# Two transformer blocks on one core: the modulation ahead of the first weights, three norm factors behind the products, and filler matmuls in front of waits

## The reference, cut to what matters

```python
mod = c_act @ w_mod + b_mod                       # 1024 x 6144; shift, scale and gate of two norms
h = rms_norm(x, norm_mix) * (1.0 + scale_m) + shift_m
z = h @ w_in                                      # first block: xr, yr, qa, ...
...
h = h + hybrid_mixer(rmsnorm(h, g_mix), ...)      # second block, layer 0 and 1; ends in y @ w_mix_out
q = rmsnorm(h, g_x) @ w_xq                        # cross attention to a memory of 256 rows, 4 heads of 256
p = softmax(q @ k.T * 256 ** -0.5);  h = h + (p @ v) @ w_xo
hn = rmsnorm(h, g_ffn)
h = h + (silu(hn @ w_gate) * (hn @ w_up)) @ w_down          # layer 0: a dense feed-forward of width 2816
h = h + sum of two chosen experts of eight, width 3584      # layer 1
```

## Time and profile before

| | us |
|---|---|
| three executions | 2289.72, 2297.3, 2298.78 |
| median | 2297.3 |
| profiled execution | 2299.69, span 2298.0 |
| mean granted TensorE clock | 0.975 of full |

### The profile page before, as it was taken

One profiled execution on the slowest core, in us unless ns is written; L12 is line 12 of the kernel. 1 busy time (PEld: TensorE's weight loads), 2 busy tenths in 40 slices (PEclk: granted clock), 3 DMA queues, 4 the chain that ended last, 5 costly groups with the idle time before them and its releaser, 6 DMA issues.

```text
span 2298.0 us, 34432 instructions
## 1 busy us (share of the span) xinstructions
PE 2179.6 (95%) x13775; PEld 1954.0 (85%) x13775; DVE 1743.8 (76%) x1916; ACT 1325.9 (58%) x1310; POOL 76.7 (3%) x160
## 2 busy tenths in 40 slices
PE   6999999999989899999888999999999999999997
PEld 3998988999978899999788888878888888888886
DVE  5768967874885555548865788888888888888887
ACT  3564434553534444435344677767777777777775
POOL 5002200000000000000000000000000000000000
PEclk9998999999999799999999999999999999999999
DMA  9646857656534346565343599999999999999995
GB/s 272 184 138 206 271 176 206 184 179 188 157 128 147 92 121 183 179 179 156 129 147 129 177 367 352 372 336 346 356 368 367 334 367 351 374 345 360 356 368 189
DMA packets 414874, 564.90 MB, mean 246 GB/s; under 512 B 17114, under 2 KB 268228, under 8 KB 414720
## 3 DMA queue, kind: packets, MB, share of 16 engines
q1 hardware_dynamic: 409680, 555.26, 71.7%
q0 software_dynamic: 5040, 7.41, 1.3%
HBM read 560.79 MB, written 1.84 MB: 245 GB/s over the span
## 4 chain that ended last, share of the span: by engine, by line
PE 81%; DVE 9%; ACT 3%; issue 2%; DVEq 0%; ACTq 0%
PE pair L1117 61%; PE misc L1117 13%; DVE arena L2042 3%; DVE wlo L1683 2%; PE misc L1592 1%; DVE wlo L2016 1%; PE pair L1560 1%; ACT whi L643 1%; PE misc L1187 1%; PE misc L1443 1%; DVE opl L1701 0%; PE misc L1171 0%; DVE rt L1708 0%; PE misc L1304 0%; PE misc L1569 0%
## 5 line engine op out<-in xcount | busy, mean ns | idle before, releaser
L2016 DVE TENSOR_TENSOR wlo<-raw,whi 128x2048 fp32r<-128x2048 f32 x336 | 764.3, 2290 | 119.3 <-ACT whi L999 118.4
L999 ACT CAST whi<-raw 128x2048 fp32r<-128x2048 f32 x336 | 643.1, 1917 | 205.0 <-PE pair L1117 123.4
L1117 PE MATMUL pair<-hh,whi 128*128 128x256 f32 x1840 | 533.3, 290 | 23.2 <-DVE hl L1701 19.6
L1683 DVE TENSOR_TENSOR wlo<-raw,whi 128x2048 fp32r<-128x2048 f32 (+1 forms) x174 | 385.2, 2216 | 193.0 <-ACT whi L643 192.4
L1117 PE MATMUL pair<-hl,whi 128*128 128x256 f32 x1840 | 527.2, 287 | 0.0
L1117 PE MATMUL pair<-hh,wlo 128*128 128x256 f32 x1840 | 527.0, 286 | 0.0
L1117 PE MATMUL pair<-whi,oph 128*128 128x512 f32 (+1 forms) x1024 | 392.3, 383 | 4.9 <-issue 4.2
L1117 PE MATMUL pair<-wlo,oph 128*128 128x512 f32 (+1 forms) x1024 | 386.5, 377 | 0.0
L1117 PE MATMUL pair<-whi,opl 128*128 128x512 f32 (+1 forms) x1024 | 386.5, 377 | 0.0
L1117 PEld LDWEIGHTS pair<-hh,whi 128*128 128x128 f32 x1840 | 360.6, 196 | 29.4 <-issue 25.5
L643 ACT CAST whi<-raw 128x2048 fp32r<-128x2048 f32 (+1 forms) x174 | 320.6, 1843 | 81.0 <-PE pair L1117 71.9
(11 more groups left out here) (440 smaller groups left out, 2450.3 us busy)
## 6 DMA issues: line engine op xcount, KB each, us to landing
raw<-in_moe_w_gate_dram SPq DMA_DIRECT2D x112, 1024.0 KB, 6.9
raw<-in_moe_w_up_dram SPq DMA_DIRECT2D x112, 1024.0 KB, 7.2
raw<-in_moe_w_down_dram SPq DMA_DIRECT2D x112, 1024.0 KB, 6.9
raw<-in_w_in_dram SPq DMA_DIRECT2D x38, 1024.0 KB, 5.9
raw<-in_w_mod_dram SPq DMA_DIRECT2D x24, 1024.0 KB, 5.6
raw<-in_w_up_dram SPq DMA_DIRECT2D x44, 512.0 KB, 5.2
raw<-in_w_xkv_dram SPq DMA_DIRECT2D x16, 1024.0 KB, 5.5
raw<-in_ffn_w_gate_dram SPq DMA_DIRECT2D x22, 512.0 KB, 4.0
```

What stands on the lines that cost most here:

```text
L999: act.copy(whi[:, q, :], raw[:, r, :]).then_inc(sem("hi_ready"), 1)
L1117: ins = pe.matmul(out_, lhs, rhs, start=start and i == 0, stop=stop and i == 2)
L1683: dve.tensor_tensor(wlo[:, i_ % SPLIT, 0:size], raw[:, raw_of(n), 0:size], whi[:, i_ % SPLIT, 0:size].bitcast(F32), ALU.subtract).then_inc ...
L2016: dve.tensor_tensor(wlo[:, q, :], raw[:, r, :], whi[:, q, :].bitcast(F32), ALU.subtract).then_inc(sem("lo_ready"), 1)
```

## The change

1. Start. All eight w_mod slots of the first norm are transferred first, then w_in. Slot 7 is shared: PE multiplies its chunks 0 to 3, DVE its chunks 4 to 7, and both are added in `mod_turned`. DVE does `mod_slot(6)` and its half of slot 7 before it copies `vec` and takes the reciprocal of the first norm. The split of the first w_in slot moves behind chunk 1 of the norm, on ACT together with the cast of the second slot.
2. x0, x1 (cross attention queries). `xT` times the gain is split straight after each group of `mixout` (`split_high` on ACT, `split_low` on DVE) into `xin`, the first 8 chunks of `oph`/`opl`; the queries go to `hh`/`hl` without the token's factor. PE sums the squares per token (`token_sums`, 16 matmuls with one column) behind the first group of `xq`. The factor, 1/16 included, is the `scale` of the exponential and multiplies the maximum.
3. ffn0. `xT` times the gain is split after each group of `xo0` into `fin` (chunks 16 to 23). PE sums the last squares behind the first group of `up2`. DVE multiplies the gate half by the factor (`gate_n`) before the silu, leaves it out of the other half, and multiplies the result of `down2` by it (`down_n`) before it adds. The output of `up2` goes to 16 chunks of `oph`/`opl` and 6 of `hh`/`hl`.
4. Fillers. `keep_busy(bank, n)` issues n float32 matmuls of `ident` by 256 columns of `spread` into a PSUM bank that nobody reads then.

```diff
-    modulator(7)
+    modulator(8)
     for j in range(4):
         dense("xr", w_in, [(XR + j * 256, 256)], "act")
-        modulator(j == 0)
...
+            def split_high(src, after, dst, gain_at):
+                for j in range(4):
+                    g = stage_groups[after][j]
+                    ahead(split_no[first_slot[g]] + len(groups[g][1]) + 1)
+                    act.wait_ge(sem("dve_read"), reads_at[g])
+                    for c in (2 * j, 2 * j + 1):
+                        act.activation(dst[:, c], src[:, c], ACT.Copy, scale=vec[:, gain_at + c:gain_at + c + 1]).then_inc(sem("h_hi"), 1)
+                    act.activation(work[:, 2 * j:2 * j + 2, :], src[:, 2 * j:2 * j + 2, :], ACT.Square).then_inc(sem("sq_ready"), 1)
...
             def high(name, shift=None):
+                    if name == "mix" and c == 1:
+                        ahead_of(stage_groups["xr"][0], 1)
...
-                norm(f"x{l}", xT, f"mixout{l}")
+                split_high(xT, f"mixout{l}", xin[0], VROW["norm_x_g_2"] + DC * l)
...
+                    if j == 1:
+                        act.wait_ge(sem("squares_summed"), SUMS.index(f"x{l}") + 1)
+                        act.activation(token_root, misc[:, 2:4, 0], ACT.Sqrt, bias=consts[:, 0:1], scale=1.0 / D)
...
-                            act.activation(sg[:, j % 3], ps[:, 0], ACT.Silu).then_inc(sem("up2_silu"), 1)
+                            act.wait_ge(sem("up2_gate"), j + 1)
+                            act.activation(sg[:, j % 3], gate_n[:, j % 3], ACT.Silu).then_inc(sem("up2_silu"), 1)
...
+            def keep_busy(bank, n):
+                for _ in range(n):
+                    pe.matmul(bank[:, 0:T], ident[:], spread[:, 0:T], start=True, stop=True)
...
             mod_turned(5)
+            for _ in range(14):
+                pe.matmul(misc[:, 3, 0:P], ident[:], ones[:], start=True, stop=True)
             mod_columns(6)
...
+                keep_busy(misc[:, 0, :], 5)
                 pe.wait_ge(sem("mix_v_normed"), 3 * (l + 1))
...
+                keep_busy(misc[:, 1, :], 8)
                 pe.wait_ge(sem("conv_taps"), 93 * (l + 1))
...
+                keep_busy(misc[:, 0, :], 5)
                 pe.wait_ge(sem("mix_sq"), 3 * l + 3)
...
                 for i, g in enumerate(stage_groups[f"xq{l}"]):
-                    dense_group(g, hh, hl, each_chunk=h_chunk(k1) if i == 0 else None)
+                    dense_group(g, *xin, each_chunk=h_chunk(k1) if i == 0 else None)
+                    if i == 0:
+                        for j in range(4):
+                            token_sums(k1, j)
...
+                keep_busy(misc[:, 0, :], 2)
                 pe.wait_ge(sem("dve_read"), reads_at[stage_groups[f"xq{l}"][-1]])
...
+                    if h == 0:
+                        pe.wait_ge(sem("root_ready"), ROOTS.index(f"x{l}") + 1)
+                        keep_busy(misc[:, 3, :], 5)
                     pe.wait_ge(sem("x_p"), 2 * (4 * l + h + 1))
...
+                    if h >= 2:
+                        keep_busy(misc[:, h % 2, :], 2)
                     pe.wait_ge(sem("x_pt_lo"), 4 * l + h + 1)
...
+            keep_busy(pair[:, pair_seq[stage_groups["xo1"][2]] % PAIRS, 0, :], 4)
             routed(3)
...
             def gather(G, first=False):
+                if first:
+                    keep_busy(misc[:, 1, :], 2)
                 pe.wait_ge(sem("m_gt"), G + 1)
...
+            mod_slot(6)
+            mod_slot(SHARED_MOD)
             dve.wait_ge(sem("pe_start"), 1)
             dve.tensor_copy(vec[:, 0:P], misc[:, 1, 0:P]).then_inc(sem("vec_ready"), 1)
             dve.wait_ge(sem("root_ready"), 1)
             link(dve.reciprocal(rt[:], rt[:]))
-            mod_slot(6)
-            ahead_of(stage_groups["xr"][0], 0)
...
+                            dve.tensor_tensor(gate_n[:, j % 3], ps[:, 0], rt[:], ALU.mult).then_inc(sem("up2_gate"), 1)
...
+                        link(dve.tensor_tensor(down_n, ps, rt[:].unsqueeze(1).to_broadcast([P, 2, T]), ALU.mult))
+                        dve.tensor_tensor(xT[:, 2 * j:2 * j + 2, :], down_n, xT[:, 2 * j:2 * j + 2, :], ALU.add)
```

More of the change, by code:

```diff
@@ L39 @@
 LATE_SPARE = (21, 22)
+SHARED_MOD = 7
+SHARED_AT = 4
 PAIRS = 2
@@ L243, in build_program @@
     pe_no = {j: i for i, j in enumerate(mod_on_pe)}
-    dve_mods = [j for j in range(24) if j not in mod_on_pe]
+    dve_mods = [j for j in range(24) if j not in mod_on_pe or j == SHARED_MOD]
     dve_no = {j: i for i, j in enumerate(dve_mods)}
@@ L358, in build_program @@
         uf = aview(2304, 3, T)
+        gate_n = aview(0, 3, T)
+        down_n = aview(768, 2, T)
         y8 = aview(0, DC, T)
@@ L953, in _ @@
                     act.copy(queries[0][:, 2 * j:2 * j + 2, :], ps).then_inc(sem("kvq_hi"), 1)
+                    if j == 1:
+                        act.wait_ge(sem("squares_summed"), SUMS.index(f"x{l}") + 1)
+                        act.activation(token_root, misc[:, 2:4, 0], ACT.Sqrt, bias=consts[:, 0:1], scale=1.0 / D)\
+                            .then_inc(sem("root_ready"), 1)
                 ahead_of(stage_groups[f"xo{l}"][0])
@@ L981, in _ @@
                 if l == 0:
-                    norm("ffn0", xT, "xo0")
+                    split_high(xT, "xo0", fin[0], VROW["norm_ffn_g_2"])
+                    act.wait_ge(sem("squares_summed"), SUMS.index("ffn0") + 1)
+                    act.activation(rt[:], misc[:, 0, 0:T], ACT.Sqrt, bias=consts[:, 0:1], scale=1.0 / D).then_inc(sem("root_ready"), 1)
                     ups2 = stage_groups["up2"]
@@ L1151, in dense_group @@
                             col = slice(m * P, (m + 1) * P)
-                            ins = three(pair[:, q, m, 0:T], wh[:, col], wl[:, col], xh[:, x], xl[:, x], start, stop)
+                            ins = three(pair[:, q, m, 0:T], wh[:, col], wl[:, col], operand(xh, x), operand(xl, x), start, stop)
                     ins.then_inc(sem("slot_used"), 1)
@@ L1169, in mod_product @@
                 pe.wait_ge(sem(f"landed{raw_of(n)}"), landed_at[n])
-                for c in range(DC):
+                chunks = SHARED_AT if j == SHARED_MOD else DC
+                for c in range(chunks):
                     ins = pe.matmul(mod_row(i)[0], cact[:, c:c + 1], raw[:, raw_of(n), c * 256:(c + 1) * 256],
-                                    start=(c == 0), stop=(c == DC - 1))
+                                    start=(c == 0), stop=(c == chunks - 1))
                 ins.then_inc(sem("mod_direct"), 1)
@@ L1197, in into_norm, with token_sums @@
                         sums(NORM[name], j - 1)
-                sums(NORM[name], 3)
+                if name != "ffn0":
+                    sums(NORM[name], 3)
+            def token_sums(k, j):
+                pe.wait_ge(sem("sq_ready"), 4 * k + j + 1)
+                for c in (2 * j, 2 * j + 1):
+                    for i in range(TB):
+                        ins = pe.matmul(misc[:, 2 + i, 0:1], work[:, c, i * P:(i + 1) * P], ones[:, 0:1],
+                                        start=(c == 0), stop=(c == DC - 1))
+                if j == 3:
+                    ins.then_inc(sem("squares_summed"), 1)
             def h_chunk(k):
@@ L1496, in _ @@
                     for i, g in enumerate(stage_groups["up2"]):
-                        dense_group(g, hh, hl, each_chunk=h_chunk(NORM["ffn0"]) if i == 0 else None)
-                    into_norm("down2", "mix1", oph, opl, each_chunk=lambda c: (sem("u2_lo"), c + 1))
+                        dense_group(g, *fin, each_chunk=h_chunk(NORM["ffn0"]) if i == 0 else None)
+                        if i == 0:
+                            sums(NORM["ffn0"], 3)
+                    into_norm("down2", "mix1", lambda c: up2_out(0, c), lambda c: up2_out(1, c),
+                              each_chunk=lambda c: (sem("u2_lo"), c + 1))
             def routed(j):
-                pe.wait_ge(sem("h_scaled"), DC * NORM["ffn1"] + 2 * j + 2)
+                pe.wait_ge(sem("h_scaled"), DC * SCALED["ffn1"] + 2 * j + 2)
                 for c in (2 * j, 2 * j + 1):
@@ L1722, in norm @@
                     scaled(c)
+                    if name == "mix" and c == 1:
+                        ahead_of(stage_groups["xr"][0], 0)
                     if c >= 1 and name != "ffn1":
@@ L1734, in mod_slot @@
                     dve.wait_ge(sem("mod_columns"), column_no[dve_mods[i - 2]] + 1)
-                for c in range(DC):
+                first = SHARED_AT if j == SHARED_MOD else 0
+                for c in range(first, DC):
                     row = raw[:, raw_of(n), c * 256:(c + 1) * 256]
-                    if c == 0:
-                        ins = dve.tensor_scalar(summed(i), row, cact[:, 0:1], None, ALU.mult)
+                    if c == first:
+                        ins = dve.tensor_scalar(summed(i), row, cact[:, c:c + 1], None, ALU.mult)
                     else:
@@ L2183, in _ @@
                 if l == 0:
-                    norm("ffn0", xT, lambda c: col("norm_ffn_g_2", c))
```

(2 more changed lines are left out.)

63 lines of the change are left out of this document (46 added, 17 removed).

## The result

The changed kernel took 2268.9 us (median of four runs, 2268.0 to 2273.8) against 2295.4 for the kernel before beside it: ratio 0.989, 95% interval 0.987 to 0.992, so 26.5 us faster. In a later set, beside its own runs of the kernel before, it was 2271.2, ratio 0.991 (0.989 to 0.992). The forecast was 2267. The profiled execution took 2268.0 us (span 2266.3, mean granted clock 0.987); the one before took 2299.7 (2298.0, 0.975), so the two traces differ by 31.7.

The account below looks back on a forecast made before the run. PE, busy 95% of the span, bounds the kernel; gains come from its waits and half-clock matmuls. Terms 7.0 + 6.4 + 6.0 + 3.9 + 8.3 - 1.9 = 29.7, about 30 us off the 2297.3 median: 2267 us, range 2255 to 2283.

Parts of the forecast that it names:

- x0 and x1: 7.0 and 6.4 forecast: Cross attention query norms: splitting unscaled activations removes PE's wait before `xq`, gaining 7.0 us in x0 and 6.4 in x1.
- The hole: PE standing still 6.42 us between the last `mixout` group and `xq` while the norm's chain runs; forecast to be removed.
- chunks 6 and 7: Last activation chunks for `xq`, needed 36 matmuls after its start; their add, casts and low parts need about 2.2 us.
- The ring of `mixout`: ACT and DVE work per `mixout` group (add, casts, squares, weight split): about 6.3 us against PE's 5.75.
- the cover of 4.3 us: Time PE works in `xq` before needing its last two chunks; forecast to just cover their 2.2 us and a late add.
- rival C: Activation and weight splits outlast a `mixout` or `xo` group, three norms keep 3 us each: 2276 us; chance 0.10.
- ffn0: 6.0 and 2.0 of clock: Norm before `up2`: 6.0 us from its removed wait and following stretch, less new work; 2.0 of clock is `xo0`'s share.
- Rival D: Slower: the `up2` ring no longer decouples its two pairs, 2.1 us more in each of 22 groups: 2313 us; chance 0.04.
- three quarters: Share taken of the 11.1 us of clock loss in mixer squares and layer 0's attention through `xo`: 8.3 us.
- The start: 3.9 forecast: Kernel start: modulation ready at about 40.6 us instead of 46.4, gaining 3.9 us, limited by w_in's fourth slot; bounds 0 to 6.
- Rival B: The fillers buy no clock, so their 8.3 us is missing: 2276 us; chance 0.16.
- rival E: Fillers run at half clock and overrun their waits, costing 8 us a layer without clock gain: 2292 us; chance 0.08.

## Why the prediction was right, by its steps

**x0 and x1: 7.0 and 6.4 forecast, 5.4 and 4.8 found.** The hole went whole, and nothing waited for chunks 6 and 7. The ring of `mixout` ran 6.19 us from add to add where I had 6.3, and the cover of 4.3 us held: rival C is refuted. 62.6 - 55.6 is the 7.0 of the forecast to the tenth. What was mis-sized is the clock: I had priced the token sums at 3.56 us (3.47 found) and the groups around them at full clock, and the stretch has a fall of 1.5 us in each layer.

**ffn0: 6.0 and 2.0 of clock, 8.7 with `down_n` counted in the mixer; 9.3 found.** Silu and copy sit between `gate_n` and the product in a ring that never reached PE's 5.75 us. Rival D, the slow side, is refuted by `x1224` in 147.13 us. `down_n` cost its 0.7 (7.2 us of hole at mix1 against 6.5). Of the 9.3, 2.7 are `xo0`, which I gave to the fillers at three quarters; the kernels without them show 13.22 as well, so it was chance in the trace of before. Without it, 6.6 stand against the 6.7 of the norm. The end of the first `up2` group cost a wait of 0.25 us, where I had 0.5.

**The start: 3.9 forecast; 5.1 in the two profiles, 3.9 (-0.7 to 7.6) alone.** The modulation stood at 40.7 us, where I had 40.6, and the low part of the second reused slot at 50.5, where I had 51.3. The mechanism was right; in the eleven profiles that have the new start the decay chain began at 109.2 to 113.6 us, against 114.5 and 115.3 in the two that have the old order.

**The fillers: 8.3 for the clock, 1.9 against.** Alone they gave 7.9, on top of the new norms 5.5 (2274.3 - 2268.9); forecast 6.4 for both together. Rival B (no clock bought) is refuted by the squares (6.68 to 3.45) and by attention 0. `xo0`'s 2.0 was not theirs. In the mixer of layer 0 they gave 2.35 from the start of the convolution on, where I had 2.4. That the table has 1.0 is a loss of 1.34 ahead of it, in the three `mixa` groups behind the hole of mix0, a place that I took to stay as it was. A smaller loss stands inside: with their waits filled, the next one, L1496, stood longest (2.6 us), `values(1)` behind it took 6.74 us at the fallen clock, and the 5 in front of the squares ended late by 0.9 (the squares' input was ready at 688.70, PE began at 689.61). In layer 0 of the second profile of the changed kernel the clock didn't fall there, the same 5 fillers ended in time, and the piece took 0.6 less. At the end they cost 3.0, not 1.9: the two at the gather ran at half clock, 0.86 us each. That is rival E's mechanism, at the one place of this kernel where it came true.

The Trainium skill, "TensorE: Matmul & The Clock Gate", section "Why this matters for your kernels", has idle gaps between bursts as what sends the array back to half clock, if they are longer than a length that it gives. For layer 1's attention the trace of before spoke against it, and I let the row decide. The kernel without fillers took 23.9 us there, so in that execution the clock fell in both layers. That doesn't settle it, for its longest wait is 3.2 us in both layers, not 2.9, while the kernel with the start alone, with 2.9, repeated the pattern of before (24.3 in layer 0, 21.0 in layer 1). So a wait of 2.9 us did both, twice each, and why layer 1 was spared isn't shown.

**The sum.** 29.7 forecast; 31.7 in the profiles, of which 5.7 lie in untouched code; 26.5 by the medians of the first set and 21.2 by those of the last. The x norms and the end were 4.3 us too good in the forecast, and nothing made that up but a start slightly better than said and the chance of `xo0`. That the time came out within 2 us of 2267 is in part luck: the forecast took its 30 us off a median of 2297.3, and the kernel before has 2292.4 to 2295.9 in the sets here, so a gain that was 3 to 9 us too large met a base that was 1.4 to 4.9 too high.

## What to carry to other kernels

A norm whose factor can be applied behind the product takes its whole chain (squares, sum, root, reciprocal, scale) out of PE's way; check the ring of the engines that split and read against one group of matmuls, for that is where it can turn into a loss. Filling a wait pays where several microseconds of matmuls follow that it keeps at full clock; leave those out behind which only a microsecond of work stands. When a stretch doesn't give what was forecast, cut it again at the place where the change starts to act: here 1.3 us were lost ahead of it, in groups that the change doesn't touch. A low clock at one place in one profile can be chance: before pricing it, look for the same place in the other layer and in another execution.

## What the runs showed of the chip that I had not expected

- The granted clock fell with PE at 5.00 of 5.00 us busy: 0.66 in 740 to 745, behind 16 float32 matmuls with one moving column (32 records, 3.47 us of them). That a stretch shows PE as busy throughout doesn't show that its clock held.
- A fall in a stretch without waits cost a nearly fixed 1.5 us of matmul time: 17.39 or 18.88 for 144 matmuls, 34.75 or 36.24 for 288, 55.6 or 57.1 for the stretch. Behind waits it cost other sums: 2.7 for the 108 matmuls of `xo0`, 1.9 to 3.2 for the squares, 1.2 to 2.7 for the three groups of `mixa`.
- A filler of 256 float32 columns takes 0.43 us at full clock and 0.86 at half, so it is dearest where the clock has already gone.
- The clock's falls move between executions of one program: the group behind the wait at L1496 in layer 0 ran at full clock in one profile of the changed kernel and took 6.74 us, with 0.72 of the clock from 680 to 685, in the other, the three groups of `mixa` took 20.24 and 18.97 us, and the kernel's two sets of runs differ by 2.4 us.
